# Differential attention on one Trainium2 core: one maximum instruction for the two maps of a head, and other PSUM banks for the second map and the output

## The reference

```python
def diff_block(start, q, k, v, past_len, lam, lam_init, subln):
    qb, Lk = q.shape[1], k.shape[1]
    mask = chunk_mask(start, qb, past_len, Lk)
    s = jnp.einsum('bqhid,bkhid->bhiqk', q, k).astype(jnp.float32) * (C_HALF ** -0.5)
    s = jnp.where(mask, s, -jnp.inf)
    p = jax.nn.softmax(s, axis=-1)
    attn = (p[:, :, 0] - lam * p[:, :, 1]).astype(v.dtype)
    o = jnp.einsum('bhqk,bkhe->bqhe', attn, v)
    return rmsnorm(o, subln) * (1.0 - lam_init)
```

## Time and profile before

| What | us |
|---|---|
| median of three runs | 1868.09 |
| lowest, highest | 1866.68, 1869.05 |
| the profiled execution, its own time | 1870.99 |
| its span | 1869.2 |
| TensorE matmul busy in the span | 1730.5 (93%) |
| VectorE busy | 1205.7 (65%) |
| ScalarE busy | 550.7 (29%) |
| GpSimd busy | 302.4 (16%) |

### The profile page before, as it was taken

The page is one execution under the profiler, slowest core; times in us unless marked ns, Lnnn a source line. Parts: engine busy times, 40 slices in busy tenths (PEclk is TensorE's granted clock), DMA queues, the critical chain, the costliest instruction groups (busy, mean ns, idle before and its releaser), DMA issues. The chain is left out here.

```text
span 1869.2 us, 20935 instructions
## 1 busy us (share of the span) xinstructions
PE 1730.5 (93%) x7518; PEld 1141.6 (61%) x7538; DVE 1205.7 (65%) x2510; ACT 550.7 (29%) x1055; POOL 302.4 (16%) x389
## 2 busy tenths in 40 slices
PE   6999999999988899999769999999998798999997
PEld 3566666688645556666345666667886455566663
DVE  3379999999444445555143799999994444455550
ACT  2276420000232233333023754200003322333330
POOL 2002422000101321111110033220001113221211
PEclk9999999999989999999979999999999899999998
DMA  5100010100502100000051000101005021000000
GB/s 171 49 23 23 23 46 23 45 23 23 197 1 90 34 24 23 23 23 23 34 172 49 23 23 23 45 23 46 26 20 198 1 90 35 23 24 23 23 23 34
DMA packets 21190, 86.32 MB, mean 46 GB/s; under 512 B 4512, under 2 KB 9120, under 8 KB 16224
## 3 DMA queue, kind: packets, MB, share of 16 engines
q1 hardware_dynamic: 21088, 84.99, 13.0%
HBM read 66.84 MB, written 18.14 MB: 45 GB/s over the span
## 5 line engine op out<-in xcount | busy, mean ns | idle before, releaser
L1233 PE MATMUL ps<-r_xn,r_w 128*128 128x384 f32 (+1 forms) x1824 | 586.1, 474 | 13.3 <-issue 8.7
L1233 PEld LDWEIGHTS ps<-r_xn,r_w 128*128 128x128 f32 x1824 | 345.4, 191 | 208.6 <-issue 20.9
L1068 DVE TENSOR_SCALAR_CACHE_REDUCE r_ix<-r_sc,smi 128x384 bf16<-128x384 f32 x434 | 405.3, 998 | 2.1
L1154 DVE TENSOR_REDUCE sm<-ps 128x1 f32<-128x384 f32 (+8 forms) x216 | 174.8, 813 | 197.6 <-PE ps L1368 107.6
L904 ACT ACTIVATE r_sc<-ps,sm 128x384 f32<-128x384 f32 (+8 forms) x216 | 169.9, 787 | 372.7 <-DVE sm L1154 371.8
L1300 PE MATMUL ps<-r_w,r_xn 128*128 128x256 f32 (+1 forms) x1152 | 251.3, 380 | 0.0
L1300 PEld LDWEIGHTS ps<-r_w,r_xn 128*128 128x128 f32 (+1 forms) x1152 | 210.9, 184 | 40.1 <-issue 5.0
L1398 PE MATMUL ps<-r_vg,r_w 128*128 128x64 f32 (+1 forms) x1184 | 156.7, 277 | 20.3 <-DVE r_w L533 10.5
L1398 PEld LDWEIGHTS ps<-r_vg,r_w 128*128 128x128 f32 (+1 forms) x1184 | 145.3, 193 | 37.7 <-DVE r_w L496 20.0
L1362 PE MATMUL ps<-r_qk,r_ix 128*128 128x128 f32 (+4 forms) x608 | 157.1, 391 | 7.5 <-ACT r_sc L904 6.0
L1381 PE MATMUL ps<-ident,r_sc 128*128 128x128 f32 (+1 forms) x720 | 117.6, 272 | 35.4 <-ACT r_w L496 17.0
(11 more groups left out here) (173 smaller groups left out, 1695.5 us busy)
## 6 DMA issues: line engine op xcount, KB each, us to landing
r_w<-w_in SPq DMA_DIRECT2D x28, 1024.0 KB, 4.8
r_xn<-w_out SPq DMA_DIRECT2D x2, 4096.0 KB, 12.7
y<-r_res SPq DMA_DIRECT2D x16, 512.0 KB, 2.9
o_k<-r_qk SPq DMA_DIRECT2D x4, 1088.0 KB, 16.1
r_vg<-x SPq DMA_DIRECT2D x8, 512.0 KB, 11.5
r_xn<-ckT SPq DMA_DIRECT2D x2, 2048.0 KB, 8.0
r_xn<-vcache SPq DMA_DIRECT2D x2, 2048.0 KB, 14.2
o_v<-r_vg SPq DMA_DIRECT2D x4, 1024.0 KB, 17.8
```

The source lines that it names most:

```text
L1068: ins = vec.tensor_scalar(unsel[t][0:rows(t), :], sc[t][0:rows(t), :], b, None, ALU.is_ge, ALU.add, accum_out=cnt[0:rows(t), c:c + 1])
L1154: vec.tensor_reduce(negm[0:r, c:c + 1], on_slot(s, w, r), X, ALU.max, negate=True)\
L1233: ins = nc.tensor.matmul(on_ring(key, cn), w[:, k, P * s + at:P * (s + 1) + at], xnT[:, k, c0:c0 + cn], start=(k == 0), stop=(k == KT - 1))
```

## The change

VectorE no longer takes a maximum for map 0 of a differential head. At map 1 it waits until both maps are filled, then reduces both with one instruction: the source is a view of two maps one step apart, the result is two columns of `negm`, and the semaphore goes up by two. A sparse head keeps its own maximum. For the two maps of a prompt tile to lie one step apart, the second place of a prompt tile moves from banks 4 and 5 to banks 2 and 3, and `mixb` from banks 2 and 3 to banks 4 and 5. The sample tile's places are unchanged. Between the sample tile and a prompt tile the places overlap in another way than before, so TensorE waits at these two borders for the map directly before as well.

```diff
-        mixb = ps[:, 2 * BANK:4 * BANK].rearrange("p (s b) -> p s b", s=2)
+        mixb = ps[:, 4 * BANK:6 * BANK].rearrange("p (s b) -> p s b", s=2)
...
             if ATT[key[1]][0] != SAMPLE and SLOT[key] % 2:
-                slot = slot[:, BANK:]
+                slot = ps[0:r, 2 * BANK:4 * BANK]
...
                             if m == 0 and i >= 1:
                                 combine(dve, link, i - 1, first[i - 1])
-                            wait_filled(dve, s)
-                            if nmap >= 4:
-                                wait_drained(dve, MAPS[nmap - 4])
-                            vec.tensor_reduce(negm[0:r, c:c + 1], on_slot(s, w, r), X, ALU.max, negate=True)\
-                               .then_inc(negm_ready, 1)
                             nmap += 1
+                            if kind == "C" and m == 0:
+                                continue
+                            pair = [("qk", i, q) for q in range(m + 1)]
+                            for q in pair:
+                                wait_filled(dve, q)
+                                if SLOT[q] >= 4:
+                                    wait_drained(dve, MAPS[SLOT[q] - 4])
+                            if m == 0:
+                                src, dst = on_slot(s, w, r), negm[0:r, c:c + 1]
+                            else:
+                                step = (3 if t == SAMPLE else 2) * BANK
+                                src = ps[0:r, 0:2 * step].rearrange("p (m n) -> p m n", m=2)[:, :, 0:w]
+                                dst = negm[0:r, c - 1:c + 1]
+                            vec.tensor_reduce(dst, src, X, ALU.max, negate=True).then_inc(negm_ready, len(pair))
...
                         if n >= 2:
                             pe.wait_ge(drained[n % 2], n // 2)
+                        if n and (ATT[key[1]][0] == SAMPLE) != (ATT[MAPS[n - 1][1]][0] == SAMPLE):
+                            wait_drained(pe, MAPS[n - 1])
```

## The result

The changed kernel takes 1954.05 us (median of four runs, 1952.75 to 1963.6) against 1868.57 us on the same chip: a ratio of 1.0467, 95% interval 1.0442 to 1.0493, some 85 us more. One of the four runs of the kernel before took 4533.47 us, stands apart and is not in the ratio; the median of the other three is 1868.09. The forecast was 1923 with a range to 1946: the sign is right, the size is not. The loss lies in the attention. From the first scores of a layer to its last head, layer 0 takes 446.8 us instead of 407.0, layer 1 454.1 instead of 408.6.

What follows compares the result with a forecast made beforehand. TensorE, busy 93% of the span, bounds the kernel, and lateness of the exponentials counts. Terms 3.4 + 9.5 + 3.7 + 7.4 + 0.1 + 3.4 = 27.5 us a layer, twice 55, gave a median of 1923 us, range 1905 to 1946.

Steps and rivals of the forecast that it cites:

- The new instruction's price: VectorE's two-result reduction priced as one pass over twice the columns: 2.43 us for w = 1088, 2.30 for 1024.
- Tile 2: Heads 0 to 3, no projection work: exponential of map 1 about 1.0 us later in three, 0.4 in one; 3.4 us.
- sample tile: Heads 8 to 11: TensorE waits longer for late exponentials and the copy behind them; 3.4 + 1.4 + 4.7 = 9.5 us.
- tile 3: Heads 17 to 19: second exponential 1.23 us later each, head 16 covered by a sparse head's transposes; 3.7 us a layer.
- borders: First differential head of tiles 0, 1, 4, 5, 6, 7: TensorE waits for the exponential freeing the first place; 7.4 us.
- The 18 heads in projection rounds at zero: Differential heads computed beside projection work: TensorE's 3.65 us of projection matmuls cover the late exponentials, so zero cost.
- Moving the banks at nothing: Moving `mixb` and the second place changes no instruction and no order on TensorE, so it was counted at nothing.
- The clock term: Longer idle times lower TensorE's clock: two score maps caught a layer at 1.7 us each, 3.4 us a layer.
- Rival 3: TensorE's clock falls much more: 10 instead of 3.4 us a layer and a little more, 1936 to 1950; chance 0.25.
- The range: Time of the changed kernel, 1905 to 1946 us; the forecast itself, 1914 to 1935, had chance 0.5.
- The rule on breaking instructions up: Where VectorE is unsaturated but makes others wait, splitting lets work end sooner; the change does the opposite. No size given.

Runs made afterwards that it cites:

- the kernels that have one part each: The change with the joint maximum in only some heads, against the kernel before: sample tile 1903.96 us, tiles 2 and 3 1902.38 us, borders 1889.57 us.
- the borders kernel: The change with the joint maximum only in the first differential head of tiles 0, 1, 4, 5, 6, 7, against the kernel before: 1889.57 us, ratio 1.0133.

## Why the prediction was wrong in size and right in sign

- **The new instruction's price: held.** 2.42 and 2.29 us against 2.43 and 2.30. (The bounds given, 2.47 and 2.28, are 0.19 us apart and not 0.15; nothing hangs on it.)
- **Tile 2 (3.4 us a layer), sample tile (9.5), tile 3 (3.7), borders (7.4): held as waits.** Together they were 48 us; TensorE's idle time grew by 46 to 49, and in the attention of the kernels that have one part each by 20.3 (sample tile, forecast 19.0), 15.8 (tiles 2 and 3, forecast 14.2) and 14.5 (borders, forecast 14.8). Two arguments were incomplete. At the borders into tiles 5, 6 and 7 the time came out (1.32 us into tile 7, forecast 1.3) but not the cause: VectorE's copy behind the joint maximum ends the wait, not the exponential, and that the two come to nearly the same time is luck. And in tile 2 I followed the second exponential to the copy for `pv`, and what TensorE waits for first is the *first* exponential, which frees the scores' place. The sizes are near (1.2 a round against 1.0).
- **The 18 heads in projection rounds at zero: nearly held.** The heads of tiles 4 to 7 did not move by more than 0.01 us; alone, the 36 cost 0.19%, no more than the banks they come with.
- **Moving the banks at nothing: near enough.** In the profiled execution the attention's two layers differ from before by +1.9 and -3.1 us, nearly all of it in where lower clock falls. The 0.28% of the timed runs goes with 12.5 us more of lower clock; whether the banks bring that stays open.
- **The clock term (3.4 us a layer, "I take two maps"): this step failed.** It measured 33 to 36 us for both layers instead of 6.8, which is 26 to 29 of the 31 us by which the forecast fell short. The price of 1.7 us for a map caught was right: tile 5 with its border to tile 6 takes 1.48 us more than before in the borders kernel, without lower clock, and 3.17 in the change, with 3.4 us of it. What was wrong was the count, and where I counted. I took the slow maps that the trace before shows in the sample tile and added some there. But tiles 2, 3 and the borders of 4 to 6, at 1.00 before apart from one stretch of 3.4 us, became places of the same kind once their rounds had idle times of 1.2 to 3.2 us, and they have 65 us of the 89 more.
- **Rival 3** had the mechanism but bounded it by the wide maps, 10 us a layer, again a count taken where the fall was already seen. Even that bound was under the 17 measured. The Trainium skill's sentence that TensorE scales its power with utilisation (Perfetto Trace Analysis, "Matmul Optimizations"), which I had set beside the upper end, points the right way: with 46 to 49 us more of idle time the lower clock went from 51 to 140 us.
- **The range** went by the sample tile and left little for tiles 2 and 3 and nothing for the borders, which together had 65 us. It was too narrow by 8 us.
- **The rule on breaking instructions up.** The Trainium skill (Perfetto Trace Analysis, "Optimizing Scalar/DVE Operations") says that where VectorE is not saturated but makes others wait, splitting instructions may let work end sooner, and that grouping can help throughput where it is saturated. The first held here: VectorE saved 8 us, TensorE lost 82.

What is left open: why a given wait brings the lower level and the next one does not. The same program has 61 us of it in layer 0 and 78 in layer 1, and 446.8 and 454.1 us of attention. The traces give the sum, not the rule. Open too is why the whole change has more lower clock than its parts together.

## What to carry to other kernels

One instruction over two tiles that are filled one after the other gives up two overlaps: with the filling of the second tile, and with whatever reads the first result; where the engine saved is idle nearly half the time, that is a pure loss. When a change adds a wait to the engine that bounds the kernel, count that engine's clock over every round that gets the wait, also where its clock was full before, and not only where the trace already shows it low: here that was 35 of 82 us. Splitting the span into the engine's busy and idle time, with the number of matmuls unchanged, separates the two causes in one row. Do it over the stretch that the edit touches: the untouched fronts alone moved by up to 11 us of busy time between traces. And look at every instruction that stands behind the longer one on its engine: here it was also a copy for another head.

## What the runs showed of the hardware

- After the same waits the lower level comes once and not the next time. These are TensorE's rows of the changed kernel at the same place, the scores of map 1 of the last differential head of tile 2, in layer 0 and in layer 1:

```profile
503.53 0.87 PE L1373 MATMUL ps<-r_qk,r_ix 128*128 128x256 f32 x4
...
1472.10 1.53 PE L1373 MATMUL ps<-r_qk,r_ix 128*128 128x256 f32 x4
```

  The waits ahead of them are alike (3.19, 1.24 and 1.61 us in one layer, 3.19, 1.22 and 1.62 in the other), yet the matmuls take 0.87 and 1.53 us.
- A dummy matmul of 1 us costs nothing where the wait is longer than it (1.6 to 3.2 us here) and 0.6 to 1.0 us where there is none. One a head cut the lower clock from 140 to 89 us and TensorE's own busy time by 20; a second one cut no more (92 us).
- A maximum over two maps with two results takes the time of one result over the same columns, 0.152 us plus 1.047 ns a column, within 0.02 us over 256 to 2176 columns.
